# Four modulation pairs of a transformer block summed by VectorE instead of multiplied by TensorE

## The reference, cut to what matters

```python
cs = jax.nn.silu(c)                                  # c: 1024 numbers
for layer in range(2):
    mod = cs @ ada_w[layer] + ada_b[layer]           # 1024 x 3072
    shift, scale, gate = jnp.split(mod, 3, axis=-1)
    h = rms_norm(x, norm_g[layer]) * (1.0 + scale) + shift
    y = even_mixer(h, ...) if layer == 0 else odd_mixer(h, ...)
    x = x + gate * y
```

## Time and profile before

| | |
|---|---|
| median of 3 runs | 1266.9 us (1266.61 to 1268.36) |
| the profiled execution, its own time | 1268.02 us |
| its span in the trace | 1266.2 us |
| granted TensorE clock, share of full | 0.998 |
| PE busy | 1241.9 us, 98% |
| DVE busy | 828.0 us, 65% |
| ACT busy | 684.1 us, 54% |
| POOL busy | 99.1 us, 8% |
| moved by DMA | 222.91 MB, 176 GB/s on average |

### The profile page before, as it was taken

One profiled execution on the slowest core, in us unless ns is written; L12 is line 12 of the kernel. 1 busy time (PEld: TensorE's weight loads), 2 busy tenths in 40 slices (PEclk: granted clock), 3 DMA queues, 4 the chain that ended last, 5 costly groups with the idle time before them and its releaser, 6 DMA issues.

```text
span 1266.2 us, 24533 instructions
## 1 busy us (share of the span) xinstructions
PE 1241.9 (98%) x10376; PEld 1123.4 (89%) x10376; DVE 828.0 (65%) x1239; ACT 684.1 (54%) x886; POOL 99.1 (8%) x83
## 2 busy tenths in 40 slices
PE   6999999999999999999999999999999999999998
PEld 5998899879999999899888888999999999888886
DVE  3667856886866969766655545766868857555533
ACT  2556446765756567245544435756567345544433
POOL 0000000000000430230000000000430130000000
PEclk9999999999999999999999999999999999999999
DMA  9867665624544433225555554544442325555552
GB/s 383 299 259 277 253 232 189 259 100 160 168 140 167 167 134 134 70 101 176 190 172 194 185 185 168 168 159 164 152 152 101 102 100 183 177 190 189 176 170 96
DMA packets 35101, 222.91 MB, mean 176 GB/s; under 512 B 3888, under 2 KB 8240, under 8 KB 9264
## 3 DMA queue, kind: packets, MB, share of 16 engines
q1 hardware_dynamic: 31104, 215.97, 48.5%
q10 hardware_dynamic: 3888, 5.38, 1.3%
HBM read 220.28 MB, written 1.05 MB: 175 GB/s over the span
## 4 chain that ended last, share of the span: by engine, by line
PE 93%; DVE 3%; DMA 2%; ACT 1%; issue 1%; SPq 0%; POOL 0%; ACTq 0%; DVEq 0%
PE pj L637 62%; PE yv L637 14%; PE sc L637 10%; PE tp L637 4%; DVE ring_rounded L751 1%; PE tp L503 1%; DMA ring<-weights 1%; DMA xT<-x_t 1%; PE tp L2003 1%; DVE att_area L580 1%; ACT att_area L534 0%; ACT probsT L1669 0%; DVE att_area L605 0%; ACT w_split L742 0%; DVE big L1876 0%
## 5 line engine op out<-in xcount | busy, mean ns | idle before, releaser
L751 DVE TENSOR_TENSOR ring_rounded<-ring,w_split 128x2048 fp32r<-128x2048 f32 x106 | 248.2, 2347 | 59.5 <-ACT w_split L742 57.3
L2240 DVE TENSOR_TENSOR ring_rounded<-ring,big_rounded 128x2048 fp32r<-128x2048 f32 x66 | 151.3, 2293 | 107.4 <-ACT big_rounded L2116 107.2
L742 ACT CAST w_split<-ring 128x2048 fp32r<-128x2048 f32 x106 | 202.2, 1908 | 31.8 <-PE pj L637 22.5
L637 PE MATMUL pj<-h_split,w_split 128*128 128x256 f32 x1264 | 172.1, 286 | 0.2 <-ACT w_split L2498 0.2
L637 PE MATMUL pj<-h_split,ring_rounded 128*128 128x256 f32 x1264 | 165.3, 281 | 1.3 <-DVE ring_rounded L751 1.3
L637 PEld LDWEIGHTS pj<-h_split,w_split 128*128 128x128 f32 x1264 | 156.2, 189 | 6.3 <-issue 5.1
L637 PEld LDWEIGHTS pj<-h_split,ring_rounded 128*128 128x128 f32 x1264 | 155.7, 188 | 2.9 <-DVE ring_rounded L751 2.1
L2116 ACT CAST big_rounded<-ring 128x2048 fp32r<-128x2048 f32 x66 | 126.2, 1911 | 50.2 <-PE pj L637 44.8
L637 PE MATMUL pj<-hT_rounded,w_split 128*128 128x256 f32 x1136 | 146.0, 280 | 0.0
L637 PEld LDWEIGHTS pj<-hT_rounded,w_split 128*128 128x128 f32 x1136 | 139.2, 188 | 0.0
L637 PE MATMUL sc<-big_rounded 128*128 128x512 f32 x176 | 67.8, 391 | 0.0
(11 more groups left out here) (379 smaller groups left out, 2127.2 us busy)
## 6 DMA issues: line engine op xcount, KB each, us to landing
ring<-weights SPq DMA_DIRECT2D x180, 1024.0 KB, 4.9
big<-weights SPq DMA_DIRECT2D x20, 1024.0 KB, 7.8
first_block<-biases ACTq DMA_DIRECT2D x26, 192.0 KB, 4.4
first_block<-biases SPq DMA_DIRECT2D x6, 192.0 KB, 10.8
xT<-x_t SPq DMA_DIRECT2D x1, 1024.0 KB, 9.7
con<-constants SPq DMA_DIRECT2D x1, 897.0 KB, 6.6
aux<-small SPq DMA_DIRECT2D x1, 832.0 KB, 10.9
out_t<-scr SPq DMA_DIRECT2D x3, 256.0 KB, 2.4
```

The costliest lines, as they stand in the source:

```text
L637: return nc.tensor.matmul(out, lhsT, rhs, start=start, stop=stop, skip_group_check=True)
L742: act.post(nc.scalar.copy(w_split[:, w % 2], ring[:, in_ring(idx)]), s["w_high"])
L751: dve.post(nc.vector.tensor_tensor(ring_r[:, at], ring[:, at], w_split[:, w % 2].bitcast(F32), ALU.subtract), s["w_low"])
L2240: dve.tell(nc.vector.tensor_tensor(w_low(t, i), w, value(w_high(i)), ALU.subtract), s["ffn_low"])
```

## The change

- The pairs `ada1_0/1`, `ada1_2/3`, `ada1_4/5` and `ada1_6/7` (shift and scale of layer 1) leave PE. They become `mod1_0` to `mod1_3` in this order, each with two pieces of 1 MB from a new array `modulations`, in another layout: for each of 8 chunks of 128 rows, 512 columns.
- DVE makes a sum for each (`dve_mod_sum`): the first chunk times its column of cs (`tensor_scalar`), and for seven more chunks chunk times column plus the sum (`scalar_tensor_tensor`), each of 128 x 512 (2 x 256 in `raw`), each waiting for the one before. After each half of a sum it signals `mod_read`.
- PE adds the 128 partitions up by four products with one column of ones (`pe_mod`), into a bank, and DVE copies 128 x 4 from it (`dve_mod_columns`).
- `MOD_SUMS` puts sums 0, 1 and 2 at the end of DVE's steps 1, 4 and 7 (the hook `between`). Sum 3 stands behind `dve_mod_gate(0)`, where `dve_mod(1)` stood; `dve_mod(1)` goes behind the copy of `mod1_3`, ahead of the third residual. The products stand in the filler of steps 3, 6 and 9, and `mod1_3` between `even_out1` and `even_out2`.
- The pairs of layer 0's gate move: `ada0_8/9` from step 0 to 2, `ada0_10/11` from 2 to 8.
- Loads: the new pieces take the three buffers in `big2`; SP issues them behind the loads named in `MOD_AFTER`, waiting for `mod_read` of the piece before in that buffer. `ada0_8` to `ada0_11` go through the ring, which changes who comes before whom in it: `even15` follows `even11` (before: `even9`), `even_out0` follows `even14` (before: `even10`), `even_out1` and `even_out2` follow `ada0_10` and `ada0_11`, `even9` follows `even13`, `even10` and `even11` follow `ada0_8` and `ada0_9`. `EARLY_BY` goes from 6 to 5.
- With `MOD_LAST` between them, the index of `even_out0` plus two is no longer `even_out2`, so in the loops behind the attention the high and low parts of `even_out2` come one turn later.
- POOL's signal `hgrn_cleared` is replaced by `constants_set`.

```diff
@@ FILL
-    "even": {-1: ["even5"], 0: ["even6", "ada0_8", "ada0_9"], 1: ["even8"], 2: ["even13", "ada0_10", "ada0_11"],
...
+    "even": {-1: ["even5"], 0: ["even6"], 1: ["even8"], 2: ["even13", "ada0_8", "ada0_9"], 3: ["even7", "mod1_0"], 4: ["even9"],
+             5: ["even10"], 6: ["even11", "mod1_1"], 7: ["even14"], 8: ["ada0_10", "ada0_11"],
+             9: ["even15", "mod1_2"]},
...
+MOD_LAST = "mod1_3"
+MOD_SUMS = {1: 0, 4: 1, 7: 2}
@@ plan
-    add("even_out", 4)
+    names.extend(("even_out0", "even_out1", MOD_LAST, "even_out2", "even_out3"))
@@ buffers
+MODS = [n for n in NAMES if "mod" in n]
+MOD_AFTER = ("even6", "even8", "even13", "even10", "even10", "even15", "even15", "even_out3")
...
+def mod_buffer(j):
+    return RING + (j + 1) % OWN
...
-        elif "ada" in name:
-            b = RING + own_n % OWN
+        elif "ada1" in name:
+            b = mod_buffer(2 * len(MODS) + own_n)
...
-EARLY_BY = 6
+EARLY_BY = 5
@@ SP
+                for j in mods_behind.get(i, ()):
+                    if j < OWN:
...
+                    else:
+                        sp.wait_ge(s["mod_read"].sem, j - OWN + 1)
+                    sp.dma_start(mod_weights(j), mod_d[j]).then_inc(landed[mod_buffer(j)], 16)
@@ new functions
+        def dve_mod_columns(dve, name):
+            b = done(dve, name)
+            at = 4 * int(name[-1])
+            free(dve, nc.vector.tensor_copy(mod_raw[:, at:at + 4], b[:, 0:4]), name)
+        def pe_mod(pe, name):
...
+            pe.eng.wait_ge(bank_free[use % NPJ], use // NPJ)
+            pe.eng.wait_ge(s["mod_read"].sem, 2 * n + 2)
+            for m in range(4):
+                last = matmul(bank_of(name)[:, m:m + 1], mod_sum(n)[:, m // 2, (m % 2) * P:(m % 2 + 1) * P],
+                              C("ones")[:, 0:1], m == 0)
+            last.then_inc(slot_done, 1)
+        def dve_mod_sum(dve, n):
...
+            for half in range(2):
...
+                for k in range(4):
...
+                    if half == k == 0:
+                        ins = nc.vector.tensor_scalar(total, part, column, None, ALU.mult)
+                    else:
+                        ins = nc.vector.scalar_tensor_tensor(total, part, column, total, ALU.mult, ALU.add)
+                    if k < 3:
+                        dve.do(ins)
+                dve.tell(ins, s["mod_read"])
@@ PE behind the attention
             for i in range(KC // 2):
+                if i == 2:
+                    pe_mod(pe, MOD_LAST)
@@ DVE
-            dve_attention(dve, "even", even_finish, cols[:, 36:37], behind=dve_diff_first)
+            def dve_sum_behind(k):
+                if k in MOD_SUMS:
+                    dve_mod_sum(dve, MOD_SUMS[k])
+            dve_attention(dve, "even", even_finish, cols[:, 36:37], between=dve_sum_behind, behind=dve_diff_first)
...
             dve_mod_gate(dve, 0)
-            dve_mod(dve, 1)
+            dve_mod_sum(dve, 3)
             for i in range(KC // 2):
+                if i == 2:
+                    dve_mod_columns(dve, MOD_LAST)
+                    dve_mod(dve, 1)
                 dve_residual(dve, "even_out", lambda ch: mod[:, 16 + ch:17 + ch], (i,))
                 dve_lows(dve, min(IDX[f"even_out{i}"] + 2, IDX["even_out3"]))
```

More of the change, by code:

```diff
@@ L130, in buffers @@
         before, uses = last.get(b, (-1, 0))
+        if "ada1" in name and own_n <= OWN:
+            before, uses = -1, uses + len([j for j in range(2 * len(MODS)) if mod_buffer(j) == b])
         out.append((b, uses + 1, before))
@@ L136 @@
 BUFFERS = buffers()
-EARLY_BY = 6
-LOADS = sorted(range(len(NAMES)), key=lambda i: (max(BUFFERS[i][2], i - EARLY_BY if i >= len(HEAD_BUFFERS) else -1), i))
+ROW = {i: row for row, i in enumerate(i for i, b in enumerate(BUFFERS) if b)}
+EARLY_BY = 5
+LOADS = sorted((i for i, b in enumerate(BUFFERS) if b),
+               key=lambda i: (max(BUFFERS[i][2], i - EARLY_BY if i >= len(HEAD_BUFFERS) else -1), i))
 in_ring = lambda idx: BUFFERS[idx][0]
@@ L634, in weights, with mod_weights, mod_last_use, mod_sum @@
             return ring[:, b] if b < RING else big2[:, (b - RING + 1) * SLOT:(b - RING + 2) * SLOT]
+        head_use = {}
+        for i_, b_ in enumerate(HEAD_BUFFERS[:BUFFERS.index(None)]):
+            head_use[b_] = (i_, BUFFERS[i_][1])
+        def mod_weights(j):
+            at = (mod_buffer(j) - RING + 1) * SLOT
+            return big2[:, at:at + SLOT]
+        def mod_last_use(b):
+            return max(j for j in range(2 * len(MODS)) if mod_buffer(j) == b) + 1
+        def mod_sum(n):
+            return raw[:, 2 * (n % 4):2 * (n % 4) + 2, 1:SEQ + 1]
         def matmul(out, lhsT, rhs, start=True, stop=True):
@@ L1896, in dve_mod_slot @@
             free(dve, ins, name)
+        def dve_mod_columns(dve, name):
[3 more added lines that the diff above has]
+        def pe_mod(pe, name):
+            n = MODS.index(name)
+            use = bank_use(name)
+            pe.eng.wait_ge(bank_free[use % NPJ], use // NPJ)
[5 more added lines that the diff above has]
+        def dve_mod_sum(dve, n):
+            if n >= 4:
+                dve.eng.wait_ge(slot_done, IDX[MODS[n - 4]] + 1)
+            total = mod_sum(n)
+            for half in range(2):
+                j = 2 * n + half
+                _, head_uses = head_use[mod_buffer(j)]
+                dve.eng.wait_ge(landed[mod_buffer(j)], 16 * (head_uses + j // OWN + 1))
+                for k in range(4):
+                    part = mod_weights(j)[:, 2 * k * SEQ:(2 * k + 2) * SEQ].rearrange("p (m t) -> p m t", t=SEQ)
+                    column = cs[:, 4 * half + k:4 * half + k + 1]
+                    if half == k == 0:
[5 more added lines that the diff above has]
+                dve.tell(ins, s["mod_read"])
         def dve_lambda(dve):
```

58 lines of the change are left out of this document (38 added, 20 removed).

## The result

The change took **1285.8 us** (median of 4, 1284.8 to 1286.6) against 1267.6 for the kernel before: 1.0143 times as long, 95% interval 1.0125 to 1.016, or 18.1 us slower. The forecast was 1279.7 us, 12.8 us slower, in a range from 1272 to 1286: the direction and most waits were as forecast, the size was short by 5 us, and the result lies just inside the upper end.

The account below looks back on a forecast made before the run. PE bounds the kernel, so DVE's lateness counts only where PE waits: -4.4 + 2.8 + 3.6 + 0.9 + 5.9 + 0.8 + 3.2 = +12.8 us, giving 1279.7 us, range 1272 to 1286.

Parts of the forecast that it names:

- PE's ledger: On PE, four modulation pairs of 1.9 us go and return as four-product groups of 0.8 us: net -4.4 us.
- sum 0, step 2: DVE's bias of pair 2 starts 4.2 us late against 1.4 slack, so PE waits 2.8 us for the low part.
- sum 1, step 5: DVE is 4.7 us late against 1.1 slack, so PE waits 3.6 us for the low part.
- copy ahead of step 6's values: Step 6's value products wait 0.9 us more for DVE's late copy of even10.
- late loads and sum 2, to `even15`: Step 7: even15's later ring load, then sum 2, delay even15's first product; 5.9 us beyond the added product.
- bank behind `even15`: Before even_out0 opens, DVE must empty the third added product's bank behind its gating: 0.8 us.
- sum 3 and ACT's order: Behind the attention: 1.4 us waiting for the last added product's bank, 1.8 for even_out2's later cast: 3.2 us.
- Rival 1: DVE's idle third hides the sums, leaving only PE's saving of 4.4 us: 1262.5 us, faster; chance 0.05.
- rival 2: DVE's fused operation runs as fast as the 427 ns row, a sum takes 3.7 us: 1269.7 us; chance 0.05.
- Rival 3: Loads of even15 and even_out0 meet other transfers and grow; at twice 4.9 us: 1284.6 us; chance 0.05.
- the load of `even_out0`: Step 7's second ring load, now following even14, is late like even15's but ends before sum 2.
- One sign of being wrong: The prediction is wrong if, among other signs, the kernel gains or loses outside 80 to 200 us.

Follow-up runs that it names:

- e1: Changed kernel, plus products of the identity with ones on PE between second and third filler block in steps 2 and 5: 1284.3 us.
- e2: Changed kernel with sums 0 and 1 at two operations a half instead of four: 1279.6 us.
- e12: The kernel before, run again unchanged with a profile of its own: 1267.1 us, ratio 0.9999.
- e3: Changed kernel with sum 2 alone cut to one operation a half, six of its eight chunks left out: 1287.2 us.
- e5: Changed kernel with sum 2 cut to one operation a half and ada0_10 loaded outside the ring: 1278.1 us.
- e6: Changed kernel with ACT casting the high part of even_out2 ahead of the first square, as before the change: 1284.0 us.
- e4: Changed kernel with only ada0_10 loaded into a separate buffer instead of the ring, sums untouched: 1284.3 us.
- e10: Changed kernel with whole sums in halves at separate places, ada0_10 out of the ring and ACT's order as before the change: 1272.8 us.

## Why the prediction was right, and where it fell short

| step of the prediction | forecast | in the change's profile |
|---|---|---|
| PE's ledger | -4.4 | -4.1 (product 0.87 us, from 111.91 to 112.78) |
| sum 0, step 2 | 2.8 | 2.79 |
| sum 1, step 5 | 3.6 | 3.49 |
| copy ahead of step 6's values | 0.9 | 0 (0.73 in e1) |
| late loads and sum 2, to `even15` | 5.9 | 5.6 |
| bank behind `even15` | 0.8 | 0.44 |
| sum 3 and ACT's order | 3.2 | 1.52 + 1.63 |
| clock behind the waits | none | 1.41 + 1.61 + 1.23 + 1.32 = 5.6 |
| behind the odd attention's first product | none | about 1 |

The fifth row is the growth of the distance between the two kernels from the scores of pair 7 (144.36 in the change, in the kernel before as below) to `even15` (162.83 against 151.62 in the earlier trace rows):

```profile
138.75 1.14 PE L637 MATMUL sc<-big 64*128 64x256 f32 x8
```

The last row is what the two first profiles differ by there, stalls of both included (17.6 us at the odd attention's first product, 210.36 against 192.80, and 18.6 at the end). The right column adds up to 17.9; the spans differ by 18.6, and the rest lies ahead of the odd attention and was not located.

**The mechanism of the waits was right**: DVE's place in the step, not its busy share, decides, and the waits of sums 0, 1 and 3 came out within 0.2 us by slack against length, the one to `even15` within 0.3. Rival 1 (the idle third of DVE hides the sums) falls with the waits and with e2, rival 2 with 753 ns. Rival 3 (late loads grow) falls for the load of `even15`, which ACT could read 4.9 us behind its issue (143.68 to 148.61); the load of `even_out0` did grow, to 6.1 (152.66 to 158.78).

**The step that failed is the sum itself**: each wait was charged at its length. The blocks behind four of them started at a granted clock of 0.50 or 0.51 and added 5.6 us, for which the sum has no term. In the kernel before PE's longest wait in the stretch was 0.57 us and its granted clock was 1.00 all through, so no row there priced a long wait, and the prediction did not ask what a wait of 3 us would do to that clock. A warning stood at the start of that trace: 32 products took 1.94 us behind a wait of 6.25 us, and 1.08 us later, though the granted clock reads 1.00 at both:

```profile
6.25 1.94 PE L637 MATMUL pj<-big,cs 128*32 128x128 f32 x32 [6.25 <-DMA big<-weights]
...
18.92 1.08 PE L637 MATMUL pj<-big,cs 128*32 128x128 f32 x32
```

The bounds (1277.2 to 1283.1) were those of prices alone and missed the result. That the range held it, by 0.2 us, is luck: rival 3 had widened it, and the clock, not the loads, made the excess. One sign of being wrong that the prediction had named did come: a loss outside 80 to 200 us, of about 1 us (e12 leaves open whose it is).

**Two smaller steps were wrong.** The load of `even_out0` does end before sum 2, but what follows it on ACT was left out: the cast ended at 160.7 and the copy behind it at 161.5, sum 2 at 162.0; e3 to e5 show that both held `even15`. It did not change the sum, but it would have sent a repair to the wrong place. And the bank that `even_out0` waits for is not that of the third added product: the banks take turns, so it is the one of `even15`, freed by DVE's gating (the wait of 0.44 us names L1922), and the product's copy is not in it.

## What to carry to other kernels

Where the busiest engine runs without gaps, work moved to an idle one is worth its price only if it fits the slack at its own place, and the slack is read as the time between that engine's end and the consumer's start, step by step. A wait of some microseconds on TensorE can cost more than its length, so price it with the blocks behind it. When a repair buys nothing, look for a second delay that ends at the same point before dropping it.

## What was not expected of the hardware

The price of a wait varied from profile to profile. Behind the same wait of 2.79 us in step 2 the third block took 3.47 us in the change, 3.67 in e6, 2.92 with a slow pair behind it (2.73) in e3, but 2.17 in e4 and 2.14 in e5. Behind 1.52 us in e6 two blocks were slow, behind 1.85 and 1.69 us in e10 none. So one such wait cost between nothing and some 3 us more than its length. That this is what spreads the executions of one kernel (1281.6 to 1285.3 in e4) is likely but not shown, since only one execution of each has a trace.
